# Four edits in a fused two-model kernel: order of the first loads, place of a softmax scale, order of decay work, place of the recurrence's bonus

## What is computed

```python
mod = silu(c) @ ada_w + ada_b                        # shift, scale, gate
h = rms_norm(x, norm_g) * (1 + scale) + shift        # hc likewise from ctx
u_sh, g_rw, u_mla, g_mla = split(h @ w_in)
# recurrence, 8 heads of 64, forward and backward; its states begin with ctx
w_log = -softplus(-(w0 + tanh(w_in) @ w2)) - 0.5;  decay = exp(-exp(w_log))
a = sigmoid(a0 + a_in @ a2);  k_dir = k * (1 + (a - 1) * k_a);  b_dir = kk * a
S = S * decay + (S @ -kk) b_dir^T + v k_dir^T;   y = S @ r
yn = (y - mean) * rsqrt(var + LNX_EPS) * lnx_g + lnx_b
bonus = sum(r * (k_dir[0] + k_dir[1]) * r_k) * v     # over the 64 of a head
rw = (yn + bonus) * silu(gate)
# attention, 8 heads, 256 queries over 512 keys, scale ATTN_SCALE = 96 ** -0.5
c_q = rms_norm(u_mla[..., :Q_LORA], q_g);  q = c_q @ w_uq, partly rotated
o = softmax(q @ k * ATTN_SCALE) @ v
x = x + gate * (concat(rw, o * silu(g_mla)) @ w_out);  x = rms_norm(x, final_g)
```

## Time and profile before

| what | value |
| --- | --- |
| median of three runs | 1221.64 us |
| lowest, highest | 1221.28, 1224.31 us |
| the profiled execution, its time | 1221.2 us |
| its span, first to last instruction | 1219.4 us |
| busy: PE, PEld, DVE, ACT, POOL | 1146.8, 798.5, 643.8, 338.6, 112.9 us |
| mean granted TensorE clock | 0.960 of full speed |

### The profile page before, as it was taken

The page is one execution under the profiler, slowest core; times in us unless marked ns, Lnnn a source line. Parts: engine busy times, 40 slices in busy tenths (PEclk is TensorE's granted clock), DMA queues, the critical chain, the costliest instruction groups (busy, mean ns, idle before and its releaser), DMA issues.

```text
span 1219.4 us, 15604 instructions
## 1 busy us (share of the span) xinstructions
PE 1146.8 (94%) x6191; PEld 798.5 (65%) x6191; DVE 643.8 (53%) x1366; ACT 338.6 (28%) x788; POOL 112.9 (9%) x107
## 2 busy tenths in 40 slices
PE   4899999989868898999999999999999999999998
PEld 2545857657768587546558888744556478888543
DVE  2222125757876855599615566650598326656400
ACT  2212223765453231523311212200525121121100
POOL 0000101200120011054000000010162000000000
PEclk9899989989788987999999999999999999999999
DMA  9723232000003202353237445423532254444410
GB/s 357 258 77 110 92 124 74 1 1 1 2 1 94 91 20 69 138 207 131 77 90 230 138 150 177 157 104 103 207 136 72 69 189 156 139 138 163 177 40 35
DMA packets 96666, 140.06 MB, mean 115 GB/s; under 512 B 12207, under 2 KB 63058, under 8 KB 96466
## 3 DMA queue, kind: packets, MB, share of 16 engines
q1 hardware_dynamic: 95684, 136.84, 33.0%
q10 hardware_dynamic: 910, 2.22, 0.5%
HBM read 138.01 MB, written 1.05 MB: 114 GB/s over the span
## 4 chain that ended last, share of the span: by engine, by line
PE 76%; DVE 17%; ACT 3%; issue 2%; DMA 1%; SPq 0%; POOL 0%; DVEq 0%; ACTq 0%
PE bank L1330 25%; PE bank L1349 12%; PE bank L815 12%; PE bank L480 2%; PE bank L473 2%; PE bank L1158 2%; DVE work L2584 1%; PE bank L620 1%; DMA ring<-in_ada_w 1%; PE bank L1092 1%; PE bank L1148 1%; DVE work L2579 1%; PE bank L1033 1%; PE bank L599 1%; PE bank L649 1%
## 5 line engine op out<-in xcount | busy, mean ns | idle before, releaser
L1330 PE MATMUL bank<-work,ring 128*128 128x256 f32 x1024 | 222.7, 379 | 0.0
L1330 PEld LDWEIGHTS bank<-work,ring 128*128 128x128 f32 x1024 | 194.2, 190 | 26.2
L815 PE MATMUL bank<-work,ring 128*128 128x256 f32 (+1 forms) x432 | 142.9, 490 | 2.3 <-ACT work L1402 2.3
L1349 PE MATMUL bank<-ring,work 128*128 128x512 f32 x288 | 124.3, 592 | 0.0
L815 PEld LDWEIGHTS bank<-work,ring 128*128 128x128 f32 x432 | 83.7, 197 | 56.9 <-issue 47.6
L1853 ACT ACTIVATE work<-work,prm 128x256 f32<-128x256 f32 x88 | 48.0, 593 | 250.5 <-DVE work L2724 224.0
L1349 PEld LDWEIGHTS bank<-ring,work 128*128 128x128 f32 x288 | 54.7, 190 | 68.0 <-issue 67.4
L2716 DVE TENSOR_TENSOR work<-bank,turned 128x512 f32<-128x512 f32 x44 | 30.4, 691 | 112.0 <-PE bank L1330 112.0
L1330 PE MATMUL bank<-work 128*128 128x256 f32 x384 | 83.9, 379 | 0.0
L1330 PEld LDWEIGHTS bank<-work 128*128 128x128 f32 x384 | 73.0, 190 | 9.9
L2734 DVE SCALAR_TENSOR_TENSOR work<-work,prm 128x256 f32<-128x256 f32 x176 | 77.1, 479 | 4.2 <-ACT work L1853 2.6
(11 more groups left out here) (454 smaller groups left out, 1758.3 us busy)
## 6 DMA issues: line engine op xcount, KB each, us to landing
ring<-in_w_up SPq DMA_DIRECT2D x32, 1024.0 KB, 7.7
ring<-in_w_in SPq DMA_DIRECT2D x24, 1024.0 KB, 7.6
ring<-in_w_down SPq DMA_DIRECT2D x16, 1024.0 KB, 6.0
ring<-in_ada_w SPq DMA_DIRECT2D x12, 1024.0 KB, 11.5
work<-in_w_up SPq DMA_DIRECT2D x12, 1024.0 KB, 7.8
ring<-in_w_out SPq DMA_DIRECT2D x10, 1024.0 KB, 7.0
work<-in_w_in SPq DMA_DIRECT2D x4, 1024.0 KB, 8.4
work<-in_w_down SPq DMA_DIRECT2D x4, 1024.0 KB, 6.0
```

What stands on the lines that cost most here:

```text
L815: ins = mm(b[0:rows, 0:toks], wt[:, k, off:off + rows], hT[:, k, 0:toks], start=(k == 0), stop=(k == KD - 1))
L1330: ins = mm(b[:, SEQ * half:SEQ * half + SEQ], wt[:, KD * half + k, P * j:P * j + P], xnT[:, k, :], start=(k == 0), stop=(k == KD - 1))
L1349: ins = mm(acc[2 * t + j][:, :], actT[:, k, P * t:P * t + P], wt[:, q, 512 * j:512 * j + 512], start=(k == 0), stop=(k == FB - 1))
```

## The change

- x and ctx are issued by SP ahead of all tiles, and no more by ACT. On PE the 32 transposes stand right behind `modulation_rows(0)`; `modulation_rows(1)` and the columns of row 0 follow. ACT squares x ahead of its copy of row 0, and copies row 1 behind its copies of `hT`.
- The loops over chunks 4 to 7: chunk 5's decays and tanh are where they were; those of chunks 6 and 7 stand in the step of chunk 4 and 5, on PE behind `reads()` and ahead of `keyed_values`, on ACT behind `take_products` and ahead of `take_keyed_values`. DVE's order is the same.
- The softmax's scale is in the queries: the variance's factor and epsilon are divided by the square of ATTN_SCALE. `row_maximum` is one operation, and the exponential has no scale.
- The bonus: `bon` lies in the second half of `vb`. DVE makes the four products behind the second inversion and the two with `v` behind `state_inputs(0)`; PE's sums are a function `bonus_sums`, called in `join_quarters(1)` between mid and corner. The last product into `mixT` is written without flattening.

The diff (eight blanks of indentation cut):

```diff
 by_column = sq_d.rearrange("p (s n) -> p s n", s=32)
-bon, yn = take_work(A0 + 5120, RB, SEQ), take_work(A0 + 6144, RB, SEQ)
+bon, yn = vb[:, :, SEQ:2 * SEQ], take_work(A0 + 6144, RB, SEQ)
 ysq = take_work(A0 + 7168, 2, 512)
...
     modulation_rows(0)
-    modulation_rows(1)
-    modulation_columns("mod", mod_rows, 0, range(4))
-
     pe.wait_ge(S["xs"], 4)
...
         ins.then_inc(*filling(("hT", k)))
+    modulation_rows(1)
+    modulation_columns("mod", mod_rows, 0, range(4))
     modulation_rows(2)
...
+    def bonus_sums():
+        pe.wait_ge(S["bonus_in"], 1)
+        for j in range(2):
+            pe.wait_ge(*turn(("bonus", j)))
+            b = bank_of(("bonus", j))
+            for i in range(2):
+                ins = mm(b[:, SEQ * i:SEQ * i + SEQ], C("half_ones"), bon[:, 2 * j + i, :], start=True, stop=True)
+            ins.then_inc(*filling(("bonus", j)))
+
     def join_quarters(p):
...
         ins.then_inc(*filling(("mid", p)))
+        if p:
+            bonus_sums()
         pe.wait_ge(*when_empty(("mid", p)))
...
         keys, tokens, reads = prepare(n)
-        if n < 7:
-            decays_and_rates(n + 1)
+        if n == 4:
+            decays_and_rates(5)
         keys()
...
         reads()
+        if n < 6:
+            decays_and_rates(n + 2)
         keyed_values(n)
...
         ins.then_inc(*filling(("gate_b", j)))
-
-    pe.wait_ge(S["bonus_in"], 1)
-    for j in range(2):
-        pe.wait_ge(*turn(("bonus", j)))
-        b = bank_of(("bonus", j))
-        for i in range(2):
-            ins = mm(b[:, SEQ * i:SEQ * i + SEQ], C("half_ones"), bon[:, 2 * j + i, :], start=True, stop=True)
-        ins.then_inc(*filling(("bonus", j)))
...
     act.dma_start(con[:, 0:N_FIRST], consts[:, 0:N_FIRST]).then_inc(S["first_consts"], 16)
-    for j, name in enumerate(("x", "ctx")):
-        act.dma_start(xc[:, 2 * j:2 * j + 2, :], w[name].rearrange("a (t p) d -> p (a t) d", p=P)).then_inc(S["x_in"], 16)
     rows = {"norm_g": w["norm_g"][0], "mu_prev": w["shift_mu"][0, 0], "mu_next": w["shift_mu"][0, 1], "w0": w["rw_w0"][0].rearrange("d n -> (d n)"),
...
         A.activation(mod_rows[:, 512 * n:512 * n + 512], b[:, :], ACT.Copy).then_inc(*emptying(("mod_row", n)))
-    take_row(0)
     act.wait_ge(S["x_in"], 32)
...
         act.wait_ge(S["ssq"], t + 1)
-    take_row(1)
+    take_row(0)
     for k in range(0, KD, 2):
...
         A.activation(hT[:, k, :], b[:, :], ACT.Copy).then_inc(*emptying(("hT", k)))
+    take_row(1)
     take_row(2)
...
             q = i % 3
-            A.activation(prob[:, q, :], b[:, :], ACT.Exp, bias=small[:, 167 + q:168 + q], scale=ATTN_SCALE,
+            A.activation(prob[:, q, :], b[:, :], ACT.Exp, bias=small[:, 167 + q:168 + q],
                                accum_out=small[:, 176 + 8 * (i % 2) + i // 2:177 + 8 * (i % 2) + i // 2]).then_inc(*emptying(("s", i)))
...
     read_growths(4)
+    tanh_rows(5)
+    key_rates(5)
     for n in range(4, 8):
-        if n < 7:
-            tanh_rows(n + 1)
-            key_rates(n + 1)
         take_blocks(n)
...
         take_products(n)
+        if n < 6:
+            tanh_rows(n + 2)
+            key_rates(n + 2)
         take_keyed_values(n)
...
         b = bank_of(("s", i))
-        V.tensor_reduce(small[:, 164 + q:165 + q], b[:, :], AX_X, MAX, negate=True).then_inc(S["vec_step"], 1)
-        vec.wait_ge(S["vec_step"], next(vec_steps))
-        TS(small[:, 167 + q:168 + q], small[:, 164 + q:165 + q], ATTN_SCALE, None, MUL).then_inc(S["m_bias"], 1)
+        V.tensor_reduce(small[:, 167 + q:168 + q], b[:, :], AX_X, MAX, negate=True).then_inc(S["m_bias"], 1)
...
     b = bank_of("lat_ssq")
-    TS(small[:, 120:122], b[:, 0:2], 1.0 / Q_LORA, EPS, MUL, ADD).then_inc(S["vec_step"], 1)
+    TS(small[:, 120:122], b[:, 0:2], ATTN_SCALE ** -2 / Q_LORA, ATTN_SCALE ** -2 * EPS, MUL, ADD).then_inc(S["vec_step"], 1)
     vec.wait_ge(S["vec_step"], next(vec_steps))
...
     invert(1, states_between)
+    for k in range(RB):
+        ins = STT(out=bon[:, k, :], in0=kds[:, k, :], scalar=col("rk", 1, k), in1=rb[:, k, :], op0=MUL, op1=MUL)
+    ins.then_inc(S["bonus_in"], 1)
     state_steps(0)
...
     state_inputs(0)
+    for j in range(2):
+        vec.wait_ge(*when_full(("bonus", j)))
+        b = bank_of(("bonus", j))
+        TT(bon[:, 2 * j:2 * j + 2, :], b[:, :].rearrange("p (a n) -> p a n", a=2), vb[:, 2 * j:2 * j + 2, 0:SEQ], MUL).then_inc(*emptying(("bonus", j)))
     for i in range(2, 4):
...
     take_read(7)
-    for k in range(RB):
-        ins = STT(out=bon[:, k, :], in0=kds[:, k, :], scalar=col("rk", 1, k), in1=rb[:, k, :], op0=MUL, op1=MUL)
-    ins.then_inc(S["bonus_in"], 1)
-
     for q, t in enumerate((1, 0)):
...
         TS(var, var, 1.0 / HEAD, LNX_EPS, MUL, ADD).then_inc(S["y_var"], 1)
-    for j in range(2):
-        vec.wait_ge(*when_full(("bonus", j)))
-        b = bank_of(("bonus", j))
-        TT(bon[:, 2 * j:2 * j + 2, :], b[:, :].rearrange("p (a n) -> p a n", a=2), vb[:, 2 * j:2 * j + 2, 0:SEQ], MUL).then_inc(*emptying(("bonus", j)))
     for q, t in enumerate((1, 0)):
...
         vec.wait_ge(S["vec_step"], next(vec_steps))
-        STT(out=mixT[:, two, :].rearrange("p a b -> p (a b)"), in0=bon[:, two, :].rearrange("p a b -> p (a b)"), scalar=0.5,
-            in1=grw[:, two, :].rearrange("p a b -> p (a b)"), op0=MUL, op1=MUL).then_inc(S["mix_rw"], 1)
+        STT(out=mixT[:, two, :], in0=bon[:, two, :], scalar=0.5, in1=grw[:, two, :], op0=MUL, op1=MUL).then_inc(S["mix_rw"], 1)
     sine_angles(0, 1)
...
         assert count[0] == P2_DMAS, count
+    for j, name in enumerate(("x", "ctx")):
+        sp.dma_start(xc[:, 2 * j:2 * j + 2, :], w[name].rearrange("a (t p) d -> p (a t) d", p=P)).then_inc(S["x_in"], 16)
     for n, (name, parts) in enumerate(tiles):
```

## The result

The kernel after took 1212.55 us (median of 8 runs, 1206.73 to 1215.25), the kernel before in the same session 1221.46 us (8 runs, 1215.54 to 1226.75). The ratio, estimated from all runs and not the quotient of the two medians, is 0.9918, 95% interval 0.9890 to 0.9947: faster by 0.8%. The forecast was 1213.6. The profiled execution of after took 1215.1 us, 1.8 over its span, and lies in the upper part of the runs; so the traces differ by 6.1 us of span, the medians by 8.9.

What follows compares the result with a forecast made beforehand. PE was the chain's link for 76% of 1219.4 us, VectorE for 17%. Terms 0 + 1.1 + 5.0 + 0.5 + 1.4 = 8.0 us gave 1213.6 us for the median, range 1209.0 to 1219.0.

Steps and rivals of the forecast that it cites:

- x first (0): Start until the first projection: x's transfers and transposes moved earlier gain 0, bounds 0.4 us lost to 0.3 us gained.
- First projection at 37.5 +- 0.4: Sign of being right, at the kernel's start: when the first projection begins, in us; past 38.5 would be wrong.
- The rival that bytes cost 5.4 us: Kernel start: 2.1 MB more stand ahead of the weights, 5.4 us lost, 2.6 left, 1219.0 us; chance 0.07.
- Scale (1.1): Attention rows beside the first inversion: removing small VectorE operations gains 1.1 us over the last six maxima, bounds 0.4 and 1.4.
- Decays (5.0): Chunks 4 to 7 of the recurrence: decays two chunks ahead remove scans' waits for tanh, gaining 5.0 us, bounds 2.8 and 12.6.
- What is late next is VectorE: Chunks 4 to 7: once the decays' waits are gone, VectorE is the next to be late; no size given.
- if it holds, 5.8; if it falls, 4.0: Chunk 5's reads: the decays gain 5.8 us if PE's clock holds there, 4.0 if it falls; 5.0 was taken.
- the long stretch at half clock ends early: Rival: PE's stretch at 0.50 from 364.0 to 377.6 runs at full clock, 6.8 us less, 1206.8 us; chance 0.12.
- VectorE becomes the bound at once: Rival: chunk 6 gains 2.8 us, everything later is given back, the join gives nothing; 1216.3 us; chance 0.15.
- Bonus in the second join (0.5): Second join: bonus products and matmuls placed in idle time gain 0.5 us, bounds -1.3 and +1.5.
- the tie: Second join: the fourth first-stage solve waits for the first bonus bank, both ready near 432.8 us; cost 0.1 us.
- End of the recurrence (1.4): End of the recurrence: without two bonus reads the second scaling waits only for GpSimd's power, gaining 1.4 us, bounds 0.8 and 2.6.

Runs made afterwards that it cites:

- e3: The kernel before with only the softmax scale moved into the queries' norm: median 1220.72 us, ratio 0.9988.
- e1: The kernel before with only x issued first and its transposes ahead of the second modulation row: median 1223.41 us, ratio 0.9996.
- e5: The kernel after with x first undone, the other three parts kept: median 1216.86 us, ratio to before 0.9945.
- e2: The kernel before with only the decays, tanh and rates two chunks ahead: median 1220.14 us, ratio 0.9959.
- e9: The kernel after with 20 unread matmuls between the bank turns of chunk 6's second half: median 1207.55 us, ratio to before 0.9892.
- e7: The kernel after with 36 unread matmuls between the bank turns of chunk 6's second half: median 1210.03 us, ratio to before 0.9899.
- e4: The kernel before with only the bonus moved into the second join, in its own buffer: median 1222.67 us, ratio 0.9999.
- e11: The kernel after with unread matmuls cut to their gaps at the start, first join, chunk 6 and end: median 1201.70 us, ratio to before 0.9848.

## Why the prediction was right, and where it was not

The time came out 1 us under the forecast, but not all steps did.

**x first (0): right for the time, wrong for its range and its observable.** "First projection at 37.5 +- 0.4" was named, and past 38.5 as a sign of being wrong; it was 40.32. The step that failed is the bound: it was worked out from bytes and from the landing at 37.2 alone, and it let the clock of the modulation chain stand. That chain sets the projection's start through ScalarE's scaled hT. Without a fill at the start it was 37.06, 39.16, 39.20, 40.32 and 40.48 with x first, mean 39.2, and 37.41, 37.48, 37.64, 40.21, 40.44 and 40.65 without, mean 39.0. In the old order it is the transposes that meet the slow stretch (5.67 us in e3, 3.69 in before), in the new one the fourth row. So the 0 was right as a mean, and the bounds should have been some 3 us to either side. The rival that bytes cost 5.4 us falls: e1 had its weights at 37.06.

**Scale (1.1): right**, 1.0 to 1.1 in nine traces.

**Decays (5.0): right against the profile of before**, 5.0 in after and 4.9 in e5, 5.8 in e2. The waits were the two named, and chunk 5's reads kept the clock in after. "What is late next is VectorE" also held: the gap before chunk 6's second half went to 4.78 us. The term is a mean of two cases, and after hit it with a third pairing: the clock held at chunk 5, but was lost from 354.5 on, 9.5 us earlier than in before. The prediction's "if it holds, 5.8; if it falls, 4.0" missed that the long stretch behind moves with it. Nor is 5.0 what the part is worth in every execution. Without it stage (b) took 51.4 to 55.9 us, by the clock alone; with it, and no fill there, 45.6 to 46.5 in five traces. The means differ by 7.4 us. That the forecast's term met the measured one owes something to the execution that was profiled.

**That the long stretch at half clock ends early** was a rival, priced at 6.8 us more. It did not in after, and the reason given against it was too weak: "the gap before it doesn't shrink"; it grew. The price was right. e9 took the stretch away by nothing but occupied time and gained 6.5 us in stage (b). It also shows that VectorE was not the bound there, against the rival "VectorE becomes the bound at once": PE at full clock moves the chain by those 6.5 us. The Trainium skill (TensorE: Matmul & The Clock Gate, A second HAM failure mode: psum-queue depth-cycling) ascribes such swings to short idle spells between groups that cycle through banks, and by it a fill in the gap should hold the clock. e7 and e9 agree: granted clock 1.00 in e7 from 331.5 to 420, in e9 from 329 to 405.

**Bonus in the second join (0.5): low by half a microsecond in after.** Stage (c) gave 1.0 in after and 0.6 alone. The corner at full clock gave 0.6, the tie cost 0.49 and not 0.1. The signs of both were forecast. Here too the clock moves the stage as much as the part does: (c) is 12.99 to 13.77 in the four traces without it and 12.63 to 13.41 in the nine with it, means 13.5 and 12.9. So 0.5 stands as a mean.

**End of the recurrence (1.4): too high**, 0.6 in after. The working stands, two of its durations do not. The second scaling came 8.15 us behind y and not 7.8, because the power took 2.01 us; that is 0.4. The transposes at half clock are another 0.4 (12.72 against 12.30). 13.31 - 12.30 = 1.0 is what the part gives at full clock. 479.61 in before is the first of two scalings run together; the first had not run beside the power there, and in after it does (471.70 to 472.38, power from 471.88). In all nine traces with the bonus moved the power is 2.00 to 2.01 us, in the four without 1.63 to 1.64. The Trainium skill (SBUF — State Buffer, Who interferes with whom) says that a VectorE operation with two inputs in SBUF contends with a GpSimd operation that reads SBUF; the scaling has two such inputs, started 0.18 us ahead of the power, and the 0.37 us agree. Such a neighbour doesn't always cost. Later in the kernel after, one that started 0.19 us behind the same power and ended within it left it at its usual 1.63 and took its own usual 0.69:

```profile
526.78 1.63 POOL L2769 TENSOR_TENSOR small<-small,con 128x8 f32<-128x8 f32 x1
526.97 0.69 DVE L2579 TENSOR_TENSOR work<-work 128x512 f32<-128x512 f32 x1
```

No run moved the scaling away from the power. That it is the cause is argued from thirteen traces and not shown by an edit.

By stages the sum is 1.0 + 5.0 + 1.0 + 0.6 = 7.6 us against 8.0 forecast. The spans of the two traces differ by only 6.1: from the first cross sum to the first reduction of y, where PE's order is the same in both, after took 37.9 us and before 36.1, with the slow stretch from 446.5 in it. The medians differ by 8.9, and the ratio's interval is 6.5 to 13.4 us. That the forecast's 8.0 and the measured 8.9 agree so closely owes something to chance: a single part gave up to 0.4% with 1% of spread between its runs, so no one of e1 to e4 can be read from its total. By their ratios the four single parts add up to 0.04 + 0.41 + 0.12 + 0.01 = 0.6% against 0.8% together, which is within the intervals.

What stays open: where the slow stretches fall in a given execution. e5 has the kernel before's start order and yet projects at 40.44, 3 us later than before. No edit here decided it except filling the idle time.

## What to carry to other kernels

Cost a moved or removed operation over its own stage, from that stage's first event to its last: the softmax's scale, 1 us, shows there to a tenth, while the total swings by 8 to 14 us from run to run. It works only where the clock is the same in both traces: a stage that nobody changed read 51.4 us in one execution and 55.9 in another, so take several traces of such a stage, of before too. When a step takes a wait off PE, list the idle times that it lengthens and the clock behind each, for the gain can come back as half speed later. An idle time that can't be closed can be filled with unread matmuls, cut to the gap's length by the traced duration of one: 36 gained 3.3 us, 20 in the same place gained 6.5.

## What was unexpected of the hardware

The slow stretches differ between executions of one order of instructions on PE. The same first 40 us, with the same instructions, had a first projection at 37.48 (before) and 40.65 (e3), at 37.06 (e1) and 40.32 (after). All of after's 8 runs lie within 8.5 us, e1's 12 within 9.6.

The clock fell also where PE was not idle. In after, PE was busy 10.88 of the 11 us from 446.5 to 457.5, mostly with matmuls of 64 rows or 64 columns, at 0.53, and 8.50 of 8.5 us before it at 1.00. The same place is at 0.53 in e11 (439.5 to 450.5). So idle time by itself does not account for every slow stretch. No run changed these matmuls, and the cause stays open. From 520 us to 2 us before the end, mostly with 128 by 256 and 128 by 512, no kernel here had a slow stretch.

A GpSimd operation on 8 columns took 0.37 us longer where a VectorE operation that the change had set free started 0.18 us ahead of it. Removing work from one queue let two operations meet that had been apart.
